# Weights laid out as one 16 KB run per partition, and the experts' up biases moved behind the activation's transposes

## The reference

```python
def expert_block(args):
    xe, e = args
    gu = xe @ w_gu[e] + b_gu[e]                    # 1024 x 2048
    x_glu = jnp.minimum(gu[:, :D_FF], SWIGLU_LIMIT)
    x_lin = jnp.clip(gu[:, D_FF:], -SWIGLU_LIMIT, SWIGLU_LIMIT)
    act = (x_lin + 1) * (x_glu * jax.nn.sigmoid(SWIGLU_ALPHA * x_glu))
    return act @ w_dn[e] + b_dn[e]                 # 1024 x 1024
```

## Time and profile before

| | us |
|---|---|
| median of 3 runs | 1868.66 (1868.22 to 1869.66) |
| the profiled execution, its own time | 1867.69 |
| its span, first to last instruction | 1865.5 |
| PE busy | 1731.2 (93%) |
| DVE, ACT busy | 421.8, 253.5 |
| read from HBM | 536.9 MB |

### The profile page before, as it was taken

How to read it: one execution, slowest core, us unless ns; L and a number is a source line. 1 busy time by engine, 2 the same in 40 slices (tenths; PEclk the granted TensorE clock), 3 DMA queues, 4 the chain that set the end, 5 groups by cost and what they waited for, 6 DMA issues and landing times.

```text
span 1865.5 us, 20554 instructions
## 1 busy us (share of the span) xinstructions
PE 1731.2 (93%) x8420; PEld 956.6 (51%) x8420; DVE 421.8 (23%) x928; ACT 253.5 (14%) x491; POOL 9.6 (1%) x6
## 2 busy tenths in 40 slices
PE   4999999599999999999999999999969999899998
PEld 3766678333333333333333333333354688788887
DVE  2304331411111111111111111111131523244401
ACT  2014330201001010010101000000121220011000
POOL 0010000000000000000000000000000000000000
PEclk9999999699999999999999999999989999999999
DMA  9554620689999999999999999999964332544300
GB/s 375 220 136 163 243 91 28 251 336 418 418 417 418 416 420 416 419 417 418 417 417 418 417 419 416 420 416 419 412 223 156 114 118 79 166 135 170 146 23 23
DMA packets 138681, 538.52 MB, mean 289 GB/s; under 512 B 16016, under 2 KB 39760, under 8 KB 101488
## 3 DMA queue, kind: packets, MB, share of 16 engines
q1 hardware_dynamic: 126416, 533.74, 71.8%
q10 hardware_dynamic: 12224, 4.19, 1.2%
HBM read 536.86 MB, written 1.05 MB: 288 GB/s over the span
## 4 chain that ended last, share of the span: by engine, by line
PE 71%; DMA 17%; DVE 5%; SPq 5%; ACT 2%; issue 1%; DVEq 0%
DMA ring<-w_gu_dram 15%; PE scores L1660 15%; PE proj L1375 9%; PE att_out L1681 9%; PE proj L1861 8%; PE proj L1383 6%; SPq L504 4%; PE proj L1872 4%; PE proj L1500 3%; PE proj L1549 3%; PE turned L1623 2%; PE scores L1649 2%; DMA ring<-w_mod_dram 2%; PE scores L1344 1%; PE scores L1465 1%
## 5 line engine op out<-in xcount | busy, mean ns | idle before, releaser
L1660 PE MATMUL scores<-ring,arena 128*64 128x512 f32 x2112 | 469.0, 593 | 19.1 <-DMA ring<-w_gu_dram 19.1
L1660 PEld LDWEIGHTS scores<-ring,arena 128*64 128x64 f32 x2112 | 150.1, 137 | 326.8 <-issue 271.4
L1681 PE MATMUL att_out<-ring,arena 128*64 128x512 f32 x1056 | 241.2, 598 | 22.7 <-ACT arena L732 22.7
L1375 PE MATMUL proj<-arena,ring 128*128 128x256 f32 x768 | 169.9, 382 | 2.6 <-DVE arena L1007 2.6
L1861 PE MATMUL proj<-arena,ring 128*128 128x256 f32 x704 | 154.5, 383 | 5.7 <-DVE arena L1173 5.7
L1375 PEld LDWEIGHTS proj<-arena,ring 128*128 128x128 f32 x768 | 145.9, 191 | 25.1 <-DVE arena L1007 3.4
L1861 PEld LDWEIGHTS proj<-arena,ring 128*128 128x128 f32 x704 | 135.2, 192 | 24.9 <-DVE arena L1173 6.1
L1681 PEld LDWEIGHTS att_out<-ring,arena 128*64 128x64 f32 x1056 | 70.0, 136 | 149.1 <-issue 118.6
L1148 DVE COPY arena<-turned 128x512 f32<-128x512 f32 x33 | 22.8, 692 | 410.7 <-PE turned L1623 410.7
L1383 PE MATMUL proj<-ring,arena 128*128 128x512 f32 x256 | 111.1, 593 | 0.0
L728 ACT ACTIVATE arena<-att_out 128x512 f32<-128x512 f32 x33 | 19.7, 598 | 590.2 <-PE att_out L1628 590.2
(11 more groups left out here) (298 smaller groups left out, 1155.1 us busy)
## 6 DMA issues: line engine op xcount, KB each, us to landing
ring<-w_gu_dram SPq DMA_DIRECT2D x132, 2048.0 KB, 24.3
ring<-w_dn_dram SPq DMA_DIRECT2D x66, 2048.0 KB, 23.3
ring<-w_in_dram SPq DMA_DIRECT2D x18, 2048.0 KB, 19.6
ring<-w_mod_dram SPq DMA_DIRECT2D x12, 2048.0 KB, 14.4
ring<-w_up_dram SPq DMA_DIRECT2D x22, 1024.0 KB, 7.5
ring<-w_down_dram SPq DMA_DIRECT2D x5, 2048.0 KB, 7.7
ring<-w_o_dram SPq DMA_DIRECT2D x2, 2048.0 KB, 10.6
ring<-w_out_dram SPq DMA_DIRECT2D x2, 2048.0 KB, 8.4
```

The lines of the kernel that those rows point to most:

```text
L1375: ins = mm(pb[:, c * T:c * T + T], W[:, k, (c0 + c) * P:(c0 + c) * P + P], src[:, k, :], start=k == 0, stop=k == K - 1)
L1660: ins = mm(AS[n][parts, :], xe[:, k % 4, k // 4, :], W[:, kk, n * D + feats.start:n * D + feats.stop], start=False, stop=k == KD - 1)
L1681: ins = mm(AO[parts, :], act_s[:, kk, s - 4, :], W[:, kk, feats], start=s == 4 and kk == 0, stop=s == 5 and kk == 3)
```

## The change

1. Every weight slot is laid out on the host: the arrays `stream1`, `stream2` and `experts` hold, for each slot and each partition, the 16 KB which go there, as one contiguous run. Each load then moves [128 partitions x 4096 floats] (2048 floats for two short ones). `w_up`'s double loads become single ones. The bytes in the ring and their order of issue stay the same, and the waits on slots too.
2. `bgu` is 1024 wide instead of 2048: rows 0 to 31 hold the gated half of the biases and rows 64 to 95 the linear half (two loads by ACT instead of one). `OHb` gets a second one-hot in rows 64 to 95 (a second DVE copy). The bias product of bank n takes rows 64n to 64n + 63 only, so the four products are 64 rows by 64 columns, one in each quadrant of the PE array, and no two neighbours in the order share row half.
3. These products move: once ahead of the first `gather`, before the loop, and then in each item behind the activation's transposes, for the next item.

```diff
-        mod_cols = [w_cols(A["w_mod"], 2048 * g, 2048 * g + 2048)[:, 2 * n:2 * n + 2, :]
-                    for g in range(3) for n in range(4)]
-        in_cols = [w_cols(A["w_in"], lo, hi) for lo, hi in W_IN_SLOTS]
...
+        stream1 = [A["stream1"][n] for n in range(N_STREAM1)]
...
-                w, n, K, N = (A["w_gu"], s, 2, 2 * D) if s < 4 else (A["w_dn"], s - 4, 4, D)
-                src = w[e].rearrange("a (k p) n -> p (a k) n", p=P)[:, K * n:K * n + K, :]
-                sp.dma_start(slot(s, K, N), src).then_inc(landed[s], 16)
+                src = A["experts"][e].rearrange("a s p n -> p (a s) n")[:, s, :]
+                sp.dma_start(ring[:, s, :], src).then_inc(landed[s], 16)
...
-            act.dma_start(bgu[0:NE, :], A["b_gu"]).then_inc(bgu_in, 16)
+            for n in range(2):
+                act.dma_start(bgu[64 * n:64 * n + NE, :], A["b_gu"][:, n * D:n * D + D]).then_inc(bgu_in, 16)
...
-                V.tensor_copy(OHb[0:NE, :], OH[:, at].to_broadcast([NE, CAP])).then_inc(ohb_ready, 1)
+                V.tensor_copy(OHb[0:NE, :], OH[:, at].to_broadcast([NE, CAP]))
+                V.tensor_copy(OHb[64:64 + NE, :], OH[:, at].to_broadcast([NE, CAP])).then_inc(ohb_ready, 1)
...
+            def up_biases():
+                for parts, feats in halves:
+                    for n in range(2):
+                        rows_ = slice(64 * n, 64 * n + 64)
+                        ins = mm(AS[n][parts, :], OHb[rows_, :], bgu[rows_, feats], start=True, stop=False,
+                                 skip_group_check=True)
+                ins.then_inc(bias_added, 1)
+
+            pe.wait_ge(ohb_ready, 1)
+            up_biases()
             pe.wait_ge(sel_ready, 1)
             gather()
...
-                pe.wait_ge(ohb_ready, i + 1)
-                for n in range(2):
-                    for parts, feats in halves:
-                        ins = mm(AS[n][parts, :], OHb[:, :], bgu[:, n * D + feats.start:n * D + feats.stop],
-                                 start=True, stop=False)
-                ins.then_inc(bias_added, 1)
                 pe.wait_ge(xe_ready, i + 1)
...
+                pe.wait_ge(ohb_ready, i + 2)
                 pe.wait_ge(actv_ready, i + 1)
                 turn(PT, act_t).then_inc(act_turned, 1)
+                up_biases()
                 pe.wait_ge(act_s_ready, i + 1)
```

More of the change, by code:

```diff
@@ L444, in two_blocks @@
         last1 = [max(n for n in range(N1) if n % RING == s) for s in range(RING)]
[L446 to L453, removed]
+        stream2 = [A["stream2"][n] for n in range(N_STREAM2)]
+        shape2 = [(KD, 512)] * 10 + [(4, D)] * 2 + [(KD, 512)] * 13 + [(4, D)] * 5 + [(2, D)]
+        UP0, DN0 = 14, 25
         N2 = len(stream2)
@@ L489, in load @@
             def load(n):
-                src = stream1[n]
                 if n >= RING:
                     sp.wait_ge(*used1[n - RING])
-                sp.dma_start(slot(n, src.shape[1], src.shape[2]), src).then_inc(landed[n % RING], 16)
+                size = int(np.prod(shape1[n]))
+                sp.dma_start(ring[:, n % RING, 0:size], stream1[n][:, 0:size]).then_inc(landed[n % RING], 16)
             sp.dma_start(xT[:], A["xT"]).then_inc(x_in, 16)
@@ L521, in _ @@
                     sp.wait_ge(*used2[n - RING])
[L522 to L528, removed]
+                size = int(np.prod(shape2[n]))
+                sp.dma_start(ring[:, n % RING, 0:size], stream2[n][:, 0:size]).then_inc(landed2[n % RING], 16)
             for c in range(2):
@@ L534, in land2 @@
         def land2(n):
-            return 16 * sum((2 if UP0 <= m < DN0 else 1) for m in range(n + 1) if m % RING == n % RING)
+            return 16 * (n // RING + 1)
         @block.gpsimd
@@ L1661, in _ @@
                                          W[:, kk, n * D + feats.start:n * D + feats.stop],
-                                         start=False, stop=k == KD - 1)
+                                         start=False, stop=k == KD - 1, skip_group_check=True)
                     ins.then_inc(up_slot, 1)
@@ L1879, in _, with slots, row_slots @@
             sum_squares(sq2, AS[0], 8)
-INPUTS = ["w_mod", "w_in", "w_out_a", "w_out_b", "w_o", "w_router", "b_gu", "b_dn", "w_gu", "w_dn"]
-RENAMED = {"w_in_2": "w_in_2", "alpha_w2": "gla_alpha_w2_2", "w_gla": "w_gla_branch_2", "w_fox": "w_fox_branch_2",
-           "w_out_2": "w_out_2", "w_up": "w_up_2", "w_down": "w_down_2"}
+INPUTS = ["w_router", "b_gu", "b_dn"]
+RENAMED = {"w_in_2": "w_in_2", "alpha_w2": "gla_alpha_w2_2"}
+def slots(w, cols):
+    k = w.shape[0] // P
+    tiles = w.reshape(k, P, -1).transpose(1, 0, 2)
+    out = []
+    for lo, hi in cols:
+        flat = tiles[:, :, lo:hi].reshape(P, -1)
+        out.append(np.pad(flat, ((0, 0), (0, SLOT - flat.shape[1]))))
+    return out
+def row_slots(w, rows_):
+    return [slots(w[lo:lo + rows_], [(0, w.shape[1])])[0] for lo in range(0, w.shape[0], rows_)]
 def kernel(**inputs):
@@ L1902 @@
     arrays |= {name: np.ascontiguousarray(get(theirs)[0]) for name, theirs in RENAMED.items()}
+    mod_slots = []
+    for g in range(3):
+        mod_slots += row_slots(get("w_mod")[0][:, 2048 * g:2048 * g + 2048], 256)
+    in_slots = slots(get("w_in")[0], W_IN_SLOTS)
+    first = mod_slots[:4] + in_slots[:5] + [in_slots[5]] + mod_slots[4:8] + [in_slots[6]] + mod_slots[8:10] + \
+        [in_slots[7]] + mod_slots[10:] + [in_slots[8]]
+    first += row_slots(get("w_out_a")[0], 512) + row_slots(get("w_out_b")[0], 512)
+    first += slots(get("w_o")[0], [(0, 512), (512, 1024)])
+    second = slots(get("w_in_2")[0], W_IN2_SLOTS)
+    second += row_slots(get("w_gla_branch_2")[0], 512) + row_slots(get("w_fox_branch_2")[0], 512)
+    second += slots(get("w_out_2")[0], [(0, 512), (512, 1024)])
+    up = get("w_up_2")[0]
+    for n in range(11):
+        pair = np.concatenate([up[:, h * FF2 + 256 * n:h * FF2 + 256 * n + 256] for h in range(2)], axis=1)
+        second += slots(pair, [(0, 512)])
+    second += row_slots(get("w_down_2")[0], 512)
+    arrays["stream1"], arrays["stream2"] = np.stack(first), np.stack(second)
+    gu = get("w_gu")[0].reshape(NE, 4, 2, P, 2 * D).transpose(0, 1, 3, 2, 4).reshape(NE, 4, P, SLOT)
+    dn = get("w_dn")[0].reshape(NE, 2, 4, P, D).transpose(0, 1, 3, 2, 4).reshape(NE, 2, P, SLOT)
+    arrays["experts"] = np.concatenate([gu, dn], axis=1)
     arrays["xT"] = features_first(get("x")[0])
```

15 lines of the change are left out of this document (7 added, 8 removed).

## The result

| | before | after |
|---|---|---|
| median of the runs, us | 1868.44 (1868.14 to 1869.66, 4 runs) | 1845.66 (1844.98 to 1846.86, 4 runs) |
| ratio of the two, with its interval | | 0.988 [0.986, 0.990] |
| the profiled execution, its own time | 1867.69 | 1846.86 |
| its span | 1865.5 | 1844.7 |

The changed kernel is 22.8 us (1.2%) faster; forecast were 24.7 us and 1844. The profiled execution happens to be the slowest of its four, so between the two traces only 20.8 us are found.

What follows compares the result with a forecast made beforehand. The prediction took the DMA time of the loop's bytes as the bound; -25.6 + 0.2 - 0.2 + 0.9 = -24.7 us gave 1843.0 for the profiled execution, median near 1844.0, range 1835 to 1859 us.

Steps and rivals of the forecast that it cites:

- Part 1: Loop's weight loads: 16 KB runs cut an item from 30.11 to 29.29 us, in all -25.6 us.
- cut to 8 KB: Loop's weight loads: bound if 16 KB runs travel as 8 KB packets, 29.75 us an item, -11.5 us.
- address pattern: Rival, expert loads: engines' parts 128 KB apart are slower; at 410 GB/s about 1886 us; chance 0.04.
- Part 2: Bias products in each item: PE's need falls to 27.5 us, worth nothing in the loop, +0.2 us in the tail.
- two abreast: Bias products in the item: bound if they run in pairs rather than four at once, PE needs 28.3 us an item.
- The tail: Last item, behind its third slot: the moved bias products show on the path there, +0.2 us.
- Loop's entry: Ahead of gather: moved biases cost 0.9 to 1.8 us, ACT's 0.6 us copy lies uncovered; net -0.2 us (-0.6 to +0.4).
- Part 3: Kernel start: rows waits behind 16 KB packets, PE starts at 19.9 us, last w_mod piece reached at 34.0; +0.9 us.
- 8 KB's rate: Rival, loop loads: 16 KB runs move at the rate of 8 KB, only w_dn gains, 1857 us; chance 0.14.
- a rate beyond the line: Rival, loop loads: half a packet's fixed part gone, 29.05 us an item, 1836 to 1837 us; faster given 0.09.
- Not abreast: Rival, bias products: quadrants do not run together, PE needs 30.1 us an item, about 1885 us; chance 0.03.
- The clock: Rival, loop: PE's longer waits drop its clock; said to stay 1.00, no change of time; no separate chance given.

Runs made afterwards that it cites:

- the full-height kernel: Changed kernel with half of each w_dn slot's bytes not loaded and bias products of 128 rows by 64 columns at the new place; 1826.08 us.

## Why the prediction was right, and where it was not

**What bounds the kernel.** Right: the DMA engines' bytes decide the loop's end. Biases alone left the time at 1868.1, runs alone gave 1845.7.

**Part 1, -25.6 us.** Measured on the loop's stretch: -23.7, the largest miss of the sum. The item is 29.365 us, not 29.29. The mechanism is right, the size of one term is off: a 16 KB packet takes 610.2 x 29.365 / 29.29 = 611.8 ns, 0.3% above the straight line through three sizes. The trace's own packet records agree: their median is 613 ns for 16 KB in the changed kernel and 314 for 8 KB in the kernel before, and packets of 4 bytes take 9 ns, near the fixed part of some 10 ns that the line gave. (The prediction's "36.7 ns per 1024 bytes" is a slip: 225.2 ns for 6144 bytes are 36.7 ns per 1000 bytes and 37.5 per 1024. The sum uses 0.03665 per byte, which is right.) The bound "cut to 8 KB" was the thing to fear, and two 8 KB DMAs show what it would have given: 1859.5, where I had 1857. The address pattern costs nothing that shows: the two-DMA kernel has it and moves 422 GB/s against the old 423. That the longer runs outside the loop are worth nothing held too: the first product behind the loop is 20.9 us earlier, the end of the span 20.8.

**Part 2, the biases.** PE's need: 27.5 forecast, 27.57 measured; the step 0.91 forecast, 1.02 measured. They do go four abreast, more or less: 1.76 us at full height against 1.02, a factor of 1.7; and the full-height kernel's 28.27 us an item is the prediction's bound for "two abreast". "Worth nothing in the loop" held. The prediction did not ask what would bound the loop without the biases; by its comparison of paces, 28.97 against 29.3, the DMA engines would. In fact PE alone paced that kernel to its end, because the lead was used up at only 0.4 us an item. A comparison of paces alone doesn't say which engine is waited for; lead divided by the difference does. The waits stood in the third slot alone, not in the second and third. The tail behind the last third slot grew from 24.07 to 24.40 us: +0.33 against +0.2.

**Loop's entry, -0.2.** Right in sign and about in size. From the start of the last 16 products ahead of it to the first up product it takes 14.23 us (364.39 to 378.62) where it took 14.35 (361.79 to 376.14): -0.1. In the second execution of the changed kernel it is 13.94 (362.75 to 376.69): -0.4. The 0.5 us that the table loses near here come before the entry. PE at the entry of the loop, beside the earlier trace rows:

```profile
371.44 1.98 PE L1630 MATMUL scores<-arena 64*64 64x512 f32 x8
373.35 3.04 PE L1611 MATMUL turned<-arena 128*64 128x512 f32 x8
...
377.20 0.66 PE L1616 MATMUL att_out<-cst,arena 128*128 128x128 f32 x4 [0.80 <-DVE arena L1118]
...
378.62 2.79 PE L1652 MATMUL scores<-ring,arena 128*64 128x512 f32 x12 [0.77 <-ACT arena L701]
```

The biases take 1.9 us, just above the upper of the two prices that I gave, and the wait of 0.77 us for ACT's copy of `xe` lies open behind them. Against both stands that `gather` now takes 3.04 us instead of 3.68, since the granted clock rises within it. The prediction named the two costs but not this return.

**Part 3, +0.9.** PE's start at 19.79 against 19.9 forecast: this mechanism is shown. The end of the `w_mod` products at +1.0 against +0.9 is in part luck, since seven executions spread over 1.5 us there. Here the Trainium skill (DMA: Bandwidth & Descriptors, section Queues, rings and completion order) says that an engine turns from queue to queue packet by packet, and that such a packet is typically some 9 to 17 descriptors. The trace agrees with the turns, and not with turns of that length for these loads. The prediction took it that by that rule the start would cost about nothing; that was not thought through, since one turn of nine long packets would add 9 x 0.30 = 2.7 us (an estimate from that page's figure), as much as was seen (15.9 against 13.1 us). So the delay does not decide, and equal counts alone don't either. The order of the packets does. The trace records start and duration of each packet of the profile, which is one run, but not its engine. Followed from each end to the next start (a reconstruction), the eight packets of 3.2 KB that `rows` has on each engine mostly stand one at a time between single 16 KB packets, and nowhere more than five in a row.

**Sum.** 1843.0 forecast for the profiled execution, 1846.86 measured, 3.9 us more: 1.9 in the loop, 1.5 in cold products (1.0 in those of the next section, 0.5 between 324 and 364 us), and 0.1 each in the start, the entry, the tail and behind the loop. Against the medians it is 1844.0 and 1845.66. The forecast execution-to-median shift of 1 us was of the kernel before and did not carry over: here the profiled one lies 1.2 us above its median. So which executions happened to be profiled makes 2.2 us, more than the miss of 1.7 in the medians.

**Rivals.** 8 KB's rate and a slower address pattern fall by the 429 GB/s, a rate beyond the line by the item of 29.365 us. "Not abreast" falls by the 1.02 us. The clock stays at 1.00 with 1.7 us of delay an item.

## What to carry to other kernels

Where a stream of weights is the bound, lay each slot out as one run per partition as long as the slot allows; the price of a packet read from two or three sizes in the same trace, carried on as a line, gave the rate here to 0.3% and the gain to a tenth of itself. Work saved on an engine that keeps just ahead of the loads is worth nothing until the loads have slack (here 0 us, and 45 us with a sixth of the bytes left out); compare paces, and also ask how long the prefetched lead lasts. Long packets on one queue delayed small loads on the other here by about one packet each. Few long runs for the constants brought them in 8.3 us earlier, but the next load in line then decided, and no gain of the whole was shown.

## What the runs showed of the hardware that I had not expected

The same 64 records behind the `w_mod` products took 15.98 us in the kernel before, 17.01 and 15.64 in two executions of the changed one, and 15.49 to 17.05 in the others. From the chain of the changed kernel, and of its second execution under another label:

```profile
41.98 17.01 PE proj L1407 x64
```

```profile
42.53 15.64 PE proj L1407 x64
```

They begin after 4.56 us of idleness, and how soon the granted clock rises differs: over 30 to 60 us it is 0.89 in the first and 0.94 in the second. That is 1.4 us by itself; partly made up by other cold products ahead of them, 0.8 us remain at 59 us (58.99 against 58.17). The second cold stretch adds more: at 324 us the two still lie 0.85 us apart (324.66 and 323.81), at the loop's first up product 1.93 (378.62 and 376.69), and at the end of the span 2.2. So nearly all of the difference between these two executions of one program lies in cold stretches ahead of the loop. A change worth 1 us of a cold stretch can't be told by four executions.
